# The second block's attention with queries in the partitions, its sums by scans on VectorE and its probabilities turned on TensorE

## What is computed

```python
z = jnp.einsum('bhqd,bhkd->bhqk', q_blk, k) * scale
causal = kpos[None, :] < qpos[:, None]
log_keep = jnp.where(causal, jax.nn.log_sigmoid(-z), 0.0)
suffix = lax.cumsum(log_keep, axis=3, reverse=True) - log_keep
a = jnp.where(causal, jnp.exp(jax.nn.log_sigmoid(z) + suffix), 0.0)
return jnp.einsum('bhqk,bhkd->bhqd', a, v)
```

## Time and profile before

| | |
|---|---|
| median of three runs | 1000.85 us |
| the profiled execution | 1003.3 us |
| its span | 1001.6 us |
| TensorE busy | 961.5 us (96%) |
| VectorE busy | 430.4 us (43%) |
| ScalarE busy | 193.8 us (19%) |
| DMA | 301 MB, 300 GB/s over the span |
| chain that ended last | TensorE 79%, DMA 15%, SyncE's queue 3% |

### The profile page before, as it was taken

The page is one execution under the profiler, slowest core; times in us unless marked ns, Lnnn a source line. Parts: engine busy times, 40 slices in busy tenths (PEclk is TensorE's granted clock), DMA queues, the critical chain, the costliest instruction groups (busy, mean ns, idle before and its releaser), DMA issues.

```text
span 1001.6 us, 15561 instructions
## 1 busy us (share of the span) xinstructions
PE 961.5 (96%) x6427; PEld 536.5 (54%) x6427; DVE 430.4 (43%) x820; ACT 193.8 (19%) x436; POOL 30.2 (3%) x92
## 2 busy tenths in 40 slices
PE   9999999999999999999999999999988888889997
PEld 8788877576666665477764533333322232333333
DVE  4566475286666666302223743722222122222214
ACT  3424344110000001223442201111101101001102
POOL 8200000000000000000000000000000000000000
PEclk9999999999999999999999899999999999999999
DMA  9436002775666689754046899999999999999995
GB/s 353 191 128 215 3 2 93 291 288 207 282 280 280 280 344 423 295 189 148 21 168 243 298 421 427 428 428 426 427 426 428 426 427 427 428 427 427 417 414 215
DMA packets 32482, 301.46 MB, mean 301 GB/s; under 512 B 6304, under 2 KB 6432, under 8 KB 14880
## 3 DMA queue, kind: packets, MB, share of 16 engines
q1 hardware_dynamic: 32272, 300.23, 73.5%
q10 hardware_dynamic: 144, 0.26, 0.1%
HBM read 299.43 MB, written 1.05 MB: 300 GB/s over the span
## 4 chain that ended last, share of the span: by engine, by line
PE 79%; DMA 15%; SPq 3%; ACT 1%; DVE 1%; issue 1%; ACTq 0%
PE PS L2088 11%; PE PS L1746 11%; PE PS L1345 11%; PE PS L1340 9%; PE PS L1795 8%; DMA slot<-in_moe_w_up_dram 8%; PE PS L2107 7%; DMA AR<-in_moe_w_up_dram 4%; PE PS L2061 3%; SPq L729 3%; PE PS L1573 2%; DMA AR<-in_moe_w_gate_dram 2%; PE PS L1694 2%; PE PS L2036 1%; PE PS L1789 1%; PE PS L1915 1%
## 5 line engine op out<-in xcount | busy, mean ns | idle before, releaser
L1746 PE MATMUL PS<-XH,slot 128*128 128x256 f32 x512 | 113.3, 379 | 1.7 <-DVE XH L2662 0.9
L1746 PEld LDWEIGHTS PS<-XH,slot 128*128 128x128 f32 x512 | 97.1, 190 | 21.3 <-issue 8.9
L1340 PE MATMUL PS<-XH,slot 128*128 128x256 f32 x432 | 97.8, 383 | 0.3 <-DMA slot<-in_w_in_dram 0.3
L1340 PEld LDWEIGHTS PS<-XH,slot 128*128 128x128 f32 x432 | 80.7, 190 | 12.9 <-issue 1.2
L2107 PE MATMUL PS<-slot,ATT 128*32 128x512 f32 x576 | 65.3, 605 | 7.9 <-DMA slot<-in_moe_w_up_dram 7.9
L1345 PE MATMUL PS<-slot,XH 128*128 128x256 f32 (+4 forms) x224 | 72.2, 477 | 0.0
L2088 PE MATMUL PS<-slot,ATT 128*32 128x512 f32 x544 | 63.7, 593 | 8.1 <-issue 3.8
L2088 PE MATMUL PS<-slot,MASKS 128*32 128x512 f32 x576 | 64.0, 594 | 0.3 <-ACT MASKS L1250 0.3
L2712 DVE SCALAR_TENSOR_TENSOR AR<-AR 128x384 f32<-128x384 f32 x112 | 59.9, 612 | 0.0
L2061 PE MATMUL PS<-AR,DIAG 128*128 128x512 f32 x120 | 57.6, 605 | 0.0
L1345 PEld LDWEIGHTS PS<-slot,XH 128*128 128x128 f32 x224 | 41.8, 190 | 26.3 <-issue 15.5
(11 more groups left out here) (484 smaller groups left out, 1217.2 us busy)
## 6 DMA issues: line engine op xcount, KB each, us to landing
slot<-in_w_ffn_dram SPq DMA_DIRECT2D x16, 2048.0 KB, 8.9
slot<-in_moe_w_gate_dram SPq DMA_DIRECT2D x16, 2048.0 KB, 35.0
slot<-in_moe_w_down_dram SPq DMA_DIRECT2D x16, 2048.0 KB, 34.6
slot<-in_moe_w_up_dram SPq DMA_DIRECT2D x14, 2048.0 KB, 31.6
AR<-in_ada_w_dram SPq DMA_DIRECT2D x16, 1536.0 KB, 14.3
AR<-in_moe_w_gate_dram SPq DMA_DIRECT2D x9, 2048.0 KB, 24.9
AR<-in_moe_w_up_dram SPq DMA_DIRECT2D x8, 2048.0 KB, 33.7
AR<-in_moe_w_down_dram SPq DMA_DIRECT2D x7, 2048.0 KB, 32.4
```

The costliest lines, as they stand in the source:

```text
L1340: ins = pe.matmul(dst, w[:, c * width + col:c * width + col + n], HT[:, c, :], start=(c == 0), stop=(c == KC - 1))
L1746: ins = pe.matmul(PS[:, b, (f % 2) * T:(f % 2 + 1) * T], slots[s][:, c * 512 + f * P:c * 512 + (f + 1) * P], HT[:, c, :], start=(c == 0), ...
```

## The change

In the attention of the second block queries lie in the partitions and keys along the columns. For the first 128 queries there are 128 keys, for the last 128 queries 256. VectorE first adds the mask to the scores into SCORED (in XN), ScalarE makes ln(1 + exp(-|z|)) into KEPT, and VectorE adds max(z, 0). The sum over later keys is a `tensor_tensor_scan` along the columns, backwards, one for each head: state = KEEP_ON x state + sp, where KEEP_ON is 1 but for two columns at which the sum begins anew. VectorE subtracts, ScalarE takes the exponential, TensorE turns the six tiles (`turn_probs`) into banks 4 and 5, and ScalarE copies them to SA. Scores use banks 2 and 3 for every pair. The output product of a pair comes one step later. NLOW, NONES and the products with them are gone. The tail is written anew. In the first block a chunk of `mixed` moves, `first_hidden` makes four chunks of group 1 before it waits for the last tile, and the next half waits for one relu.

```diff
@@ constants: GpSimd, VectorE @@
-            pool.memset(NONES[:, :], -1.0)
-            pool.memset(NLOW[:, :], -1.0)
-            pool.affine_select(out=NLOW[:, :], in_=NLOW[:, :], compare_op=ALU.is_ge, fill=0.0, base=0,
-                               pattern=[[-1, P]], channel_multiplier=1).then_inc(ready, 1)
+            step(dve.memset(KEEP_ON, 1.0))
+            for first in (0, T):
+                dve.memset(KEEP_ON[:, first:first + 1], 0.0)
@@ ScalarE @@
+            def score_logs(t):
+                act.wait_ge(sems["sb_masked"], t + 1)
+                logs = KEPT[:, t % 2]
+                step(act.activation(logs, SCORED[:, t % 2], ACT.Abs))
+                step(act.activation(logs, logs, ACT.Exp, scale=-1.0))
+                act.activation(logs, logs, ACT.Ln, bias=EPSC[:, 1:2]).then_inc(sems["sp_ln"], 1)
+            def probs(t):
+                act.wait_ge(sems["sa_arg"], t + 1)
+                act.activation(SCORED[:, t % 2], SCORED[:, t % 2], ACT.Exp).then_inc(sems["sb_probs"], 1)
+            def take_turned_probs(t):
+                act.wait_ge(sems["sb_turned"], t + 1)
                 if t >= 2:
                     act.wait_ge(sems["sb_out"], t - 1)
+                act.activation(SA[:, t % 2], PS[:, slice(*TURN_BANKS), 0:3 * P], ACT.Copy).then_inc(sems["sa_ready"], 1)
+            def take_attended(t):
+                act.wait_ge(sems["sb_out"], t + 1)
+                act.activation(YT[:, t, :], PS[:, OUT_BANKS[t % 2], 0:T], ACT.Copy).then_inc(sems["sb_out_copied"], 1)
+            for t in range(NPAIR):
+                if t >= 2:
+                    probs(t - 2)
+                take_qk(t, 0)
+                if t >= 3:
+                    take_attended(t - 3)
+                if t >= 1:
+                    score_logs(t - 1)
+                take_qk(t, 1)
+                if t >= 2:
+                    take_turned_probs(t - 2)
+            for t in range(NPAIR - 2, NPAIR):
+                probs(t)
+                if t < NPAIR - 1:
+                    take_attended(t - 1)
+                    score_logs(t + 1)
+                take_turned_probs(t)
+                take_attended(t)
@@ TensorE, first block @@
-            mixed(1, 0, 6, 7)
+            mixed(1, 0, 6)
             within_tile(1)
             nsa_turn(0, "s")
             nsa_turn(0, "w")
             nsa_turn_compressed(0)
+            mixed(1, 0, 7)
             nsa_output(0)
...
                 turn_tile("t1_11", XR, 1, 1)
+                hidden_chunks(0, 1, 0, 4, hidden_bank(0, 0), opens=False)
                 wait_emptied(pe, "t1_01")
                 wait_emptied(pe, "t1_11")
                 for f in range(4):
-                    ins = hidden_chunks(0, f, 4 if f % 2 == 0 else 0, KC, hidden_bank(0, f // 2))
+                    ins = hidden_chunks(0, f, 4 if f < 3 else 0, KC, hidden_bank(0, f // 2))
...
-            hidden_half(1, 0, 0)
+            hidden_half(1, 0, 0, taken=1)
@@ TensorE, second block @@
-                if t >= 2:
-                    pe.wait_ge(sems["sa_arg"], t - 1)
-                for kt in range(NT):
+                else:
+                    pe.wait_ge(sems["sb_masked"], t)
+                for qt in range(NT):
                     for h in range(2):
                         p0 = h * HD
-                        ins = pe.matmul(PS[:, SCORE_BANKS[t % 2][0] + h, kt * T:kt * P + T], SQK[p0:p0 + HD, t % 3, 1, kt * P:(kt + 1) * P],
-                                        SQK[p0:p0 + HD, t % 3, 0, kt * P:T], start=(kt == 0), stop=True, skip_group_check=True)
+                        ins = pe.matmul(PS[:, SCORE_BANKS[0] + h, qt * P:(2 * qt + 1) * P], SQK[p0:p0 + HD, t % 3, 0, qt * P:(qt + 1) * P],
+                                        SQK[p0:p0 + HD, t % 3, 1, 0:(qt + 1) * P], start=(qt == 0), stop=True, skip_group_check=True)
+            def turn_probs(t):
+                pe.wait_ge(sems["sb_probs"], t + 1)
+                if t >= 1:
+                    pe.wait_ge(sems["sa_ready"], t)
                 for h in range(2):
+                    for j in range(3):
+                        ins = pe.transpose(PS[:, TURN_BANKS[0] + h, j * P:(j + 1) * P], SCORED[:, t % 2, h, j * P:(j + 1) * P], IDENT[:, :])
+                ins.then_inc(sems["sb_turned"], 1)
...
             for t in range(NPAIR):
                 query_or_key(t, 0)
-                if t >= 2:
-                    score_sums(t - 2)
+                if t >= 3:
+                    attend(t - 3)
                 if t >= 1:
                     scores(t - 1)
                 query_or_key(t, 1)
                 if t >= 2:
-                    attend(t - 2)
+                    turn_probs(t - 2)
...
-            score_sums(last - 1)
+            pe.wait_ge(sems["qk_taken"], 2 * NPAIR - 1)
+            mix_when_copied(0, 0, 1)
+            attend(last - 2)
             scores(last)
-            pe.wait_ge(sems["sb_out_copied"], NPAIR - 2)
-            mix_out(0, 1, 0, NPAIR - 2)
+            mix_when_copied(0, 1, last - 2)
+            turn_probs(last - 1)
+            mix_when_copied(0, last - 2, last - 1)
             attend(last - 1)
-            score_sums(last)
-            pe.wait_ge(sems["qk_taken"], 2 * NPAIR)
-            mix_out(1, 1, 0, NPAIR - 2)
+            mix_when_copied(1, 0, last - 1)
+            turn_probs(last)
+            mix_when_copied(0, last - 1, last)
             attend(last)
-            pe.wait_ge(sems["sb_out_copied"], NPAIR - 1)
+            mix_when_copied(1, last - 1, last)
             for n in range(2):
-                mix_out(n, 1, NPAIR - 2, NPAIR - 1)
-            pe.wait_ge(sems["sb_out_copied"], NPAIR)
-            for n in range(2):
-                mix_out(n, 1, NPAIR - 1, NPAIR).then_inc(filled, 1)
+                mix_when_copied(n, last, NPAIR).then_inc(filled, 1)
@@ VectorE @@
-            for t in range(1, NPAIR + 2):
...
-                    stt(SA[:, t % 2], score_banks(t), 0.0, bc(SBNEG[:, :, :].rearrange("p k q -> p (k q)"), 1, 2),
-                        ALU.min, ALU.add).then_inc(sems["sa_arg"], 1)
...
+            for t in range(NPAIR):
+                dve.wait_ge(sems["sb_scored"], t + 1)
                 if t >= 2:
+                    dve.wait_ge(sems["sb_turned"], t - 1)
+                scored, kept = SCORED[:, t % 2], KEPT[:, t % 2]
+                tt(scored, PS[:, slice(*SCORE_BANKS), 0:3 * P], bc(SBNEG[:, :, :].rearrange("p k q -> p (k q)"), 1, 2), ALU.add)\
+                    .then_inc(sems["sb_masked"], 1)
+                dve.wait_ge(sems["sp_ln"], t + 1)
+                step(stt(kept, scored, 0.0, kept, ALU.max, ALU.add))
+                for h in range(2):
+                    back = kept[:, h, ::-1]
+                    ins = dve.tensor_tensor_scan(back, KEEP_ON, back, 0.0, ALU.mult, ALU.add)
+                step(ins)
+                tt(scored, scored, kept, ALU.subtract).then_inc(sems["sa_arg"], 1)
```

More of the change, by code:

```diff
@@ L129, in build @@
         MASKS = sb("MASKS", [P, 4 * P])
-        UPI, UPS, NLOW, NONES = (MASKS[:, k * P:(k + 1) * P] for k in range(4))
+        UPI, UPS = (MASKS[:, k * P:(k + 1) * P] for k in range(2))
         ONES = sb("ONES", [P, P])
@@ L245, in build @@
         four = lambda v: v.rearrange("p (j h q) -> p j h q", j=2, h=2)
-        SAB = four(XN[:, :, :].rearrange("p a b -> p (a b)")[:, 0:12 * P])
-        SPB = four(carve(6 * T, 12 * P))
+        SCORED = four(XN[:, :, :].rearrange("p a b -> p (a b)")[:, 0:12 * P])
+        KEPT = four(carve(6 * T, 12 * P))
         assert 6 * T + 12 * P <= 4096
-        SCORE_BANKS = ((2, 4), (4, 6))
+        SCORE_BANKS, TURN_BANKS = (2, 4), (4, 6)
         OUT_BANKS = (0, 1)
@@ L786, in _ @@
             pool.affine_select(out=UPS[:, :], in_=UPS[:, :], compare_op=ALU.is_gt, fill=0.0, base=0,
[L787 to L789 removed]
+                               pattern=[[1, P]], channel_multiplier=-1).then_inc(ready, 1)
             part = IDENT[:, :].rearrange("p (k f h r) -> p k f h r", k=2, f=2, h=2)
@@ L1747, in hidden_chunks @@
                                     slots[s][:, c * 512 + f * P:c * 512 + (f + 1) * P], HT[:, c, :],
-                                    start=(c == 0), stop=(c == KC - 1), skip_group_check=True)
+                                    start=(opens and c == 0), stop=(c == KC - 1), skip_group_check=True)
                 return ins
```

58 lines of the change are left out of this document (10 added, 48 removed).

## The result

| | before | after |
|---|---|---|
| median of four runs each, same chip | 1000.88 us (1000.61 to 1000.97) | 987.18 us (986.39 to 988.92) |
| ratio, 95% interval | | 0.9855 (0.9836 to 0.9874) |
| profiled execution, its span | 1003.3, 1001.6 us | 988.92, 987.2 us |
| TensorE, VectorE, ScalarE busy | 961.5, 430.4, 193.8 us | 950.5, 447.0, 199.8 us |

The kernel is 13.7 us faster, where 10.9 were forecast (989.9 us, range 985.5 to 995).

A forecast was written before the change was run, and what follows sets the result against it. TensorE's issue was taken to bound the head-pair loop, and expert-weight DMA the later stretch, starting when TensorE's work has passed. Terms 8.6 + 0.1 - 0.3 + 2.5 = 10.9 us off 1000.85 gave 989.9 us, range 985.5 to 995.

The forecast's parts named there:

- Part 1: Loop over head pairs, TensorE: 1.83 us of sums leave, six transposes at 0.75 enter; 8.6 us won over eight pairs.
- rival (c): Transposes on TensorE cost their whole length, 1.6 us: gain 4.1 in all, 996.7 us; chance 0.05.
- Part 2: Loop, VectorE: scans 1.02 us each, chain 7.7 us under the 9.6 us period by 1.9, so nothing waits.
- The 4.5 us to spare: Loop: probabilities ready about 13.7 us after their pair's query slot began, turned at 18.2.
- rival (a): VectorE's scans slow: loop bound from 1.95 us a scan, gain gone at 2.7; 1009 us at 3.35; chance 0.03.
- Part 3: Attention's tail: old 0.94 us wait goes, 0.85 for pair 6's output product comes, +0.1; last pair's release moves 0.86 less.
- The old wait: Opening of the tail before the change: TensorE stands 0.94 us at 514.79 because VectorE is late.
- the 0.3 charged for it: Loss in us for the last pair's DMA release moving 0.86 us less than the rest, mostly covered by stream holes.
- The main assumption: After the attention: bring TensorE's work forward and the saturated expert stream, and so the end, comes forward by the same amount.
- Part 4: First block: three TensorE waits of 0.86, 0.88 and 0.78 us filled or removed, 2.5 us won, lower end 0.9.
- rival (b): Granted clock, 555 to 561.6 us: if the shifted program keeps it, 3 us more won, 987 us; chance 0.12.
- The downward price of (b): Transposes let the loop's clock fall to 1.2 GHz: 9.6 us a pair, 998 us for one, 1008 for two; chance 0.03.

The follow-up runs named there:

- scans_twice: The changed kernel with each pair's two scans run once more into scratch ahead of the real ones: 994.98 us, ratio 0.9940 to the kernel before.
- gate_late: The changed kernel with its first expert transfer held back until four more output projection chunks are done: 987.92 us beside 988.43 of the changed kernel.
- gate_old: The changed kernel with its first expert transfer held back until output tile so00 is done: 990.78 us, again 990.64 beside 987.38 of the changed kernel.
- scans_thrice: The changed kernel with each pair's two scans run two more times into scratch: 1010.05 us, ratio 1.008 to the kernel before.

## Why the prediction was right, point by point

**Part 1, sums out, transposes in: right in kind, too small.** The forecast said 8.6 us of a period of 9.6. The transposes took 0.65 for the 0.75 that I took above the row's 0.65; the lower end was the right value, and the allowance for "the wait that now stands before them" had nothing behind it. Also, 10.69 - 9.42 = 1.27 us left each period, 1.83 - 0.65 = 1.18 of them the exchange and 0.1 the key product, whose slot went from 3.65 to 3.56 us. That was not in the sum; from the trace it is only seen that transposes stand behind it now where the output product stood. Eight times 1.27 is 10.2. The reading of 0.11 us between starts against a record of 0.27 held, and with it went rival (c), whose price of 1.6 us a pair is not even reached by twelve transposes.

**Part 2, VectorE follows: right, by its own numbers.** Scans 0.94 for 1.02 us, extrapolated from two short rows; the chain 7.5 for 7.7; the slack before the mask 1.9 for 1.9. That the last agrees to a few hundredths is luck: chain and period (9.42 for 9.6) were each 0.2 too long. The 4.5 us to spare between the probabilities and their turning are 4.5 in the trace (497.12 to 501.60); the 13.7 and 18.2 us there count from the query slot of the step that makes the pair's scores, one period after its own. `scans_twice` shows that the slack is real and no more than that: 1.95 us used it up. The condition of rival (a) (1.95 us a scan binds the loop, 2.7 ends the gain) was tried from both sides, with scans of 1.9 and 2.8 us in effect: +5.4 us in the attention at the first, slower than before by 9 at the second. The 1.95 was too high for two reasons: with the period of 9.42 it would have been (9.42 - 5.7) / 2 = 1.86, and when VectorE no longer idles, an exponential and two copies get ahead of ScalarE's logs.

**Part 3, the tail: the wait was over-sized, the release mis-thought.** No wait is marked for pair 6's output product. Counted from the end of the last key product (501.60), the mask of pair 7 was in at 4.9 and the copy of the turned pair 6 done at 8.6, where the forecast had 5.15 and 9.0; and TensorE's chunk ahead of that output product ended its turn at 8.4 for 8.2. From a chunk's start to the output product behind it there are 1.06 us at three places of the tail where two records of this width are 0.87 apart, so at most 0.2 each is lost to ScalarE's copy, 0.6 in all for the 0.85 forecast. The old wait was worth 1.02 by starts (in the earlier trace rows the output product at 512.97 takes its usual 0.80, and the next start is at 514.79), not the 0.94 marked. So 0.4 were won where the forecast had 0.1. With part 1 this makes 10.2 + 0.4 = 10.6; measured 10.46. The release did come 0.85 us less early than the rest, as forecast (87.32 us from the first query product for 96.93, 9.61 against 10.46), but the 0.3 charged for it cost nothing: `gate_late` held it back another 2.8 us at no cost that shows.

**The main assumption: right in sign, with the wrong event.** "Bring that work forward and the stream, and so the end, comes forward" held, as the table shows. But the step that named the release of the last pair as the link failed: the first expert's transfers can go out 2.8 us later for nothing, and the end stays where the rank products put it. Only at 9.7 us of delay are 3 lost, and there it is open whether the stream or TensorE sets the end. It made little difference to this forecast, since the change moves both events nearly alike: in the profiled pair the release by 12.8 us and the rank products by 15.3, of which 1.67 are the clock and 0.85 the chunk behind the last pair.

**Part 4, three waits: 3.0 for 2.5.** The forecast took the idle times of the records (0.88, 0.78), where the starts show 1.05 and 1.01.

**What was missed beyond that** is 1.67 us at the sum banks in the profiled pair of executions. It was rival (b), whose price of 3 us is nearly what the full clock gives (19.5 - 16.6 = 2.9), but which came and went between executions of one kernel. It need not be part of the difference of the medians: attention and waits together make 13.5, and the medians differ by 13.7, 13.0 and 14.4 us in the three groups. Against that 13.5 the forecast of 10.9 was 2.6 short: 1.8 in the attention, 0.5 in the first block and 0.3 charged for the release. The downward price of (b) was added up wrong: 9.6 us on 989.9 give 999.5 and 1009, not 998 and 1008; no fall in the loop of the changed kernel was seen.

## What to carry to other kernels

Price a wait and a short instruction from start to start, with the spacing that the same record has where nothing is waited for: the marked idle times were up to a quarter short here, and the length of a transpose's record was 2.5 times its price. When work is handed from the busy engine to an idle one, lay the chain of that engine out from its first to its last use of the shared buffer and compare it with the new period; the two terms so found were within 0.2 us here, and it is the tail without cover that pays most when the slack is gone. To say which event the end hangs on, take what is left from each candidate to the end over several executions and keep the one that stays constant, here within 1.7 us against 10; then look whether the stream still has holes, for without them the constant can be a coincidence, as it may be in `gate_old`.

## What of the hardware had not been expected

The granted clock at the same instruction of the same program differed between executions (eight records of 512 columns in 3.68, 5.38 or 6.20 us in three profiles of the changed kernel), and it is worth up to 2.9 us here. At about 100 us, in the first block, it differs in the same way: one run of 86 records of 64 columns takes 2.72 us in the first two profiles of the changed kernel and 3.79 in the third. In `scans_thrice` it fell, to 0.56 and 0.54 over stretches of 3 and 7 us, after two of three waits of 2.15 us, where the loop otherwise keeps 1.00. A backward scan over 384 float32 columns costs as much as one step of twice as many columns with two inputs (0.94 and 0.96 us); the Trainium skill, page "DVE: opcode table, instruction layouts, handler registers and perf-mode slots", section "6. Datapath and trigger behaviour", has it that the built-in scan runs at half throughput, and these rows agree.
